# First four levels of a triangular inverse: 128x128 products against stacked 32x32 blocks

## The reference

```python
lower = jnp.where(strict, jnp.einsum('bhncd,bhnmd->bhncm', k_beta, k) * decay, 0.0)
a_mat = lower + jnp.eye(C, dtype=jnp.float32)
rhs = jnp.concatenate([v_beta, k_beta * jnp.exp(g)[..., None]], axis=-1)
sol = lax.linalg.triangular_solve(a_mat, rhs, left_side=True, lower=True, unit_diagonal=True)
```

## Time and profile before

| | |
|---|---|
| median of 3 runs | 1993.72 us (1990.28 to 1998.13) |
| the profiled execution | 1995.55 us |
| its span | 1993.7 us |
| PE busy | 1885.1 us, 95% |
| DVE busy | 1487.0 us, 75% |
| ACT busy | 1073.9 us, 54% |
| POOL busy | 223.7 us, 11% |
| instructions | 30396 |

### The profile page before, as it was taken

How to read it: one execution, slowest core, us unless ns; L and a number is a source line. 1 busy time by engine, 2 the same in 40 slices (tenths; PEclk the granted TensorE clock), 3 DMA queues, 4 the chain that set the end, 5 groups by cost and what they waited for, 6 DMA issues and landing times.

```text
span 1993.7 us, 30396 instructions
## 1 busy us (share of the span) xinstructions
PE 1885.1 (95%) x12080; PEld 1666.1 (84%) x12080; DVE 1487.0 (75%) x2335; ACT 1073.9 (54%) x1753; POOL 223.7 (11%) x182
## 2 busy tenths in 40 slices
PE   6899999988999998999799989998999999989998
PEld 5899788788978887888699978887888789988887
DVE  4655699866567997888777777998787777776565
ACT  5534645564365456555644556445656654456554
POOL 0210111112001111111000001111111100001111
PEclk9999999989999999999899999999999999999999
DMA  5222689522339973555443348894445433344552
GB/s 222 97 107 106 254 342 356 187 104 88 106 110 357 355 277 138 232 211 211 190 149 110 147 169 315 344 362 182 175 174 190 169 127 128 119 178 148 190 186 89
DMA packets 53277, 383.80 MB, mean 193 GB/s; under 512 B 5904, under 2 KB 6032, under 8 KB 6928
## 3 DMA queue, kind: packets, MB, share of 16 engines
q1 hardware_dynamic: 53136, 381.86, 50.9%
HBM read 380.79 MB, written 1.05 MB: 192 GB/s over the span
## 4 chain that ended last, share of the span: by engine, by line
PE 76%; DVE 12%; ACT 6%; issue 4%; DMA 2%; POOL 0%; SPq 0%; DVEq 0%; ACTq 0%
PE quad L492 19%; PE quad L493 10%; PE quad L482 6%; PE quad L483 6%; PE quad L484 6%; PE works L504 4%; PE works L506 4%; PE works L505 4%; ACT w_hi L958 2%; DVE w_lo L1272 2%; DVE mx L1391 2%; DMA raw<-w 2%; DVE mx L1432 1%; PE works L663 1%; PE works L876 1%
## 5 line engine op out<-in xcount | busy, mean ns | idle before, releaser
L1272 DVE TENSOR_TENSOR w_lo<-raw,w_hi 128x1024 fp32r<-128x1024 f32 x572 | 700.5, 1233 | 239.0 <-ACT w_hi L958 237.7
L492 PE MATMUL quad<-h_two,w_hi 128*128 128x512 f32 x2112 | 750.8, 399 | 15.6 <-DVE h_two L1280 9.7
L958 ACT ACTIVATE w_hi<-raw 128x1024 fp32r<-128x1024 f32 x572 | 596.1, 1054 | 206.3 <-PE quad L493 89.9
L493 PE MATMUL quad<-h_two,w_lo 128*128 128x256 f32 x2112 | 594.0, 281 | 0.0
L492 PEld LDWEIGHTS quad<-h_two,w_hi 128*128 128x128 f32 x2112 | 398.1, 189 | 116.9 <-issue 19.7
L493 PEld LDWEIGHTS quad<-h_two,w_lo 128*128 128x128 f32 x2112 | 400.4, 190 | 1.9
L1773 POOL TENSOR_TENSOR g_lo<-hid,g_hi 128x256 fp32r<-128x256 f32 x140 | 177.6, 1270 | 1550.9 <-ACT g_hi L988 1550.9
L482 PE MATMUL quad<-h_two,w_hi 128*128 128x256 f32 x960 | 279.0, 291 | 6.1 <-DVE w_lo L1272 6.1
L483 PE MATMUL quad<-h_two,w_hi 128*128 128x256 f32 x960 | 273.3, 285 | 0.0
L484 PE MATMUL quad<-h_two,w_lo 128*128 128x256 f32 x960 | 273.2, 285 | 0.0
L482 PEld LDWEIGHTS quad<-h_two,w_hi 128*128 128x128 f32 x960 | 185.8, 194 | 9.5 <-issue 8.2
(11 more groups left out here) (404 smaller groups left out, 2355.6 us busy)
## 6 DMA issues: line engine op xcount, KB each, us to landing
raw<-w SPq DMA_DIRECT2D x294, 1024.0 KB, 4.9
mx<-w SPq DMA_DIRECT2D x64, 1024.0 KB, 7.0
par<-p_in SPq DMA_DIRECT2D x2, 1110.0 KB, 7.0
x<-x_in SPq DMA_DIRECT2D x1, 1024.0 KB, 6.6
mx<-bt_in SPq DMA_DIRECT2D x2, 512.0 KB, 5.7
out<-x SPq DMA_DIRECT2D x4, 256.0 KB, 2.5
con<-const_in SPq DMA_DIRECT2D x1, 780.0 KB, 4.6
par<-p_in SPq DMA_DIRECT2D x1, 225.0 KB, 6.8
```

Of the source, the lines that this page charges most:

```text
L492: mm(o, hi, h_two[:, kt, :, :], start=kt == 0, stop=False, skip_group_check=True)
L493: return mm(o[:, 0:T], lo, h_hi[:, kt, :], start=False, stop=kt == DT - 1, skip_group_check=True)
L958: f(w_hi[:, v % SLOTS, :], raw[:, chunk_of_unit[v] % RAWS, (v % 2) * UNIT:(v % 2 + 1) * UNIT], ACT.Copy).then_inc(s_hi_ready, 1)
L1272: v.tensor_tensor(w_lo[:, q % SLOTS, :], raw[:, chunk_of_unit[q] % RAWS, (q % 2) * UNIT:(q % 2 + 1) * UNIT], w_hi[:, q % SLOTS, :].bitcast ...
```

## The change

The first four levels never leave the 32x32 blocks on the diagonal. The new code stacks these: `lt_c`, `xi_c`, `xt_c`, `tt_c` are 128 x 8 x 32, with the diagonal block of quarter q of each matrix on the partitions of that quarter.

- `kk`: DVE copies the four quarters of `lt` into `lt_c`, masks, forms I - mask on 128x256, and makes `xt_c` by a block transpose. Step `level` is gone on PE and ACT. POOL makes all four masked copies at once (128x256 each), and then sets `xt` and half of `x` to zero.
- `lvt`, levels 1 to 4: 32 products of 32x32 into one bank, the quarter as the inner loop; one ACT copy of 128x256.
- `lvx`, levels 1 to 4: 32 products 32x32 with 16 columns, for `xt` alone; DVE subtracts on 128x128 and gets `xi_c` by a block transpose.
- The wait for `s_qk_done` moves from lvt 1 to lvt 5.
- Level 5 reads the stacked blocks. Meanwhile POOL copies the blocks (six copies 32x256, each behind the one before) to their places in `xt` and in `xi64`; lvt 6 waits for four of them and the scan for all.
- `con` has five 32-column masks and a 32-column identity in place of seven 128-column masks.

```diff
-                elif kind == "level":
-                    for c in range(TT):
-                        pe.wait_ge(s_x0_done, 2 * L + c + 1)
-                        pe.wait_ge(s_lt_done, 2 * L + c + 1)
-                        for h, r, cols in heads(c):
-                            last = tr(work[c][:, cols], xi[:, r, :], ident)
-                        last.then_inc(s_pe_x0, 1)
                 elif kind == "lvt" and i < 5:
...
+                    pe.wait_ge(s_pool_lts, 4 * L + i)
+                    if i == 1:
+                        pe.wait_ge(s_x0_done, L + 1)
+                    else:
+                        pe.wait_ge(s_x_upd, 8 * L + i - 1)
+                    for r in range(8):
+                        for q in quarter:
+                            last = mm(work[0][q, 32 * r:32 * r + 32], lts_c[i - 1][q, r, :], xt_c[q, r, :],
+                                      start=True, stop=True)
+                    last.then_inc(s_pe_t, 1)
                 elif kind == "lvx" and i < 5:
...
+                    pe.wait_ge(s_t_sb, 8 * L + i)
+                    if i > 1:
+                        pe.wait_ge(s_xi_ready, 4 * L + i - 1)
+                    o = work[1][:, 0:P].rearrange("p (r g b) -> p r g b", r=8, b=1 << i)
+                    for r in range(8):
+                        for q in quarter:
+                            odd = tt_c[q, r, :].rearrange("p (g e b) -> p g e b", e=2, b=1 << i)[:, :, 1, :]
+                            last = mm(o[q, r], xi_c[q, r, :], odd, start=True, stop=True)
+                    last.then_inc(s_pe_dx, 1)
...
+                elif kind == "lvt" and i < 5:
+                    act.wait_ge(s_pe_t, 8 * L + i)
+                    f(A["t"][:, 0:T], work[0][:, 0:T], ACT.Copy).then_inc(s_t_sb, 1)
...
+                    dve.wait_ge(s_lt_done, 2 * (L + 1))
+                    for q in quarter:
+                        v.tensor_copy(lt_c[q], lt[q, :, q]).then_inc(s_ltc_done, 1)
+                    dve.wait_ge(s_ltc_done, 4 * (L + 1))
+                    v.tensor_tensor(xi_c, lt_c, c_("m", 0, 32).unsqueeze(1).to_broadcast([P, 8, 32]), ALU.mult)\
+                        .then_inc(s_l0_masked, 1)
+                    dve.wait_ge(s_l0_masked, L + 1)
+                    link(v.scalar_tensor_tensor(xi_c, xi_c, -1.0, c_("idc").unsqueeze(1).to_broadcast([P, 8, 32]),
+                                                ALU.mult, ALU.add))
+                    v.transpose(xt_c, xi_c).then_inc(s_x0_done, 1)
...
+                elif kind == "lvx" and i < 5:
+                    dve.wait_ge(s_pe_dx, 8 * L + i)
+                    dve.wait_ge(s_x0_done, L + 1)
+                    odd = xt_c.rearrange("p r (g e b) -> p r g e b", e=2, b=1 << i)[:, :, :, 1, :]
+                    v.tensor_tensor(odd, odd, work[1][:, 0:P].rearrange("p (r g b) -> p r g b", r=8, b=1 << i),
+                                    ALU.subtract).then_inc(s_x_upd, 1)
+                    dve.wait_ge(s_x_upd, 8 * L + i)
+                    v.transpose(xi_c, xt_c).then_inc(s_xi_ready, 1)
...
+                elif kind == "kk":
+                    pool.wait_ge(s_ltc_done, 4 * (L + 1))
+                    for lev in range(1, 5):
+                        v.tensor_tensor(lts_c[lev - 1], lt_c,
+                                        c_("m", 32 * lev, 32 * lev + 32).unsqueeze(1).to_broadcast([P, 8, 32]), ALU.mult)\
                             .then_inc(s_pool_lts, 1)
+                    v.memset(A["xt"], 0.0).then_inc(s_zeroed, 1)
+                    v.memset(A["x"][:, 0:512], 0.0).then_inc(s_zeroed, 1)
+                elif kind == "lvt" and i == 5:
+                    pool.wait_ge(s_zeroed, 2 * (L + 1))
+                    pool.wait_ge(s_x_upd, 8 * L + 4)
+                    pool.wait_ge(s_xi_ready, 4 * (L + 1))
+                    pool.wait_ge(s_qdec_done, L + 1)
+                    for k, (dst, src) in enumerate([(xt[q, :, q], xt_c[q]) for q in quarter[2:]]
+                                                   + [(xi64[q, :, q], xi_c[q]) for q in quarter[:2]]
+                                                   + [(xt[q, :, q], xt_c[q]) for q in quarter[:2]]):
+                        v.tensor_copy(dst, src).then_inc(s_spread, 1)
+                        pool.wait_ge(s_spread, 6 * L + k + 1)
```

More of the change, by code:

```diff
@@ L70 @@
      ("pair", 3), ("lead", 8), ("silu", 3), ("pair", 8), ("lead", 9), ("nsum", 1), ("pair", 9), ("nroot", 1),
-     ("nrow", 1), ("lead", 4), ("kk", 0), ("nrow", 0), ("pair", 4), ("level", 0), ("kq", 0), ("lead", 5),
+     ("nrow", 1), ("lead", 4), ("kk", 0), ("nrow", 0), ("pair", 4), ("kq", 0), ("lead", 5),
      ("silu", 4), ("lvt", 1), ("tokk", 0), ("pair", 5), ("lvx", 1), ("lead", 10), ("silu", 5), ("lvt", 2),
@@ L202 @@
                   ("d", 4), ("b_re", 4 * P), ("b_im", 4 * P), ("c_re", ST * 32), ("c_im", ST * 32)])
-PC, NC = columns([("ident", P), ("triu", P), ("ones", P), ("m", 7 * P), ("pen", P), ("time", T // 2), ("c", 8),
+PC, NC = columns([("ident", P), ("triu", P), ("ones", P), ("m", 5 * 32), ("idc", 32), ("pen", P), ("time", T // 2), ("c", 8),
                   ("final", 8), ("sel", 8)])
@@ L315, in build @@
         qdec = hf[:, 2:4, :].rearrange("p n t -> p (n t)").rearrange("p (n t) -> p n t", t=P)
+        blocks = lambda a: a.rearrange("p (n t) -> p n t", t=32)
+        xi64 = A["x"][:, 0:512].rearrange("p (n t) -> p n t", t=64)
+        tt6 = A["t"][:, 0:512].rearrange("p (n t) -> p n t", t=64)
+        xi_c, xt_c = blocks(A["x"][:, 512:768]), blocks(A["x"][:, 768:1024])
+        tt_c, lt_c, tt5 = (blocks(A["t"][:, k:k + T]) for k in (0, 256, 512))
+        lts_c = [blocks(A["lts"][:, T * k:T * k + T]) for k in range(4)]
+        quarter = [slice(32 * p, 32 * p + 32) for p in range(4)]
         vn0, s_sb = lts[:, 0:4, :], lts[:, 4:8, :]
@@ L377, in build @@
             conv_done th_done silu_done rt_done rs_done pe_nrow qk_ready pe_kk lt_done
-            pe_kq qk_done l0_masked x0_done pe_tokk pe_tokv kd_done vb_done pool_lts
-            pe_x0 x0_sb pe_t t_sb pe_dx
+            pe_kq qk_done l0_masked x0_done ltc_done xi_ready zeroed spread pe_tokk pe_tokv kd_done vb_done pool_lts
+            pe_t t_sb pe_dx
             x_upd z_th c_done pe_u0 vn0_done pe_s s_done pe_w w_done pe_u1
@@ L772, in _ @@
                         for r in range(8):
-                            last = mm(works[up, 2 * p, 32 * r:32 * r + 32], lt[low, r, up], xt[low, r, low],
+                            last = mm(works[up, 2 * p, 32 * r:32 * r + 32], lt[low, r, up], xt_c[low, r, :],
                                       start=True, stop=True)
@@ L1131, in _ @@
                                 .then_inc(s_kd_done, 1)
[L1132 to L1135, removed]
+                elif kind == "lvt" and i < 5:
+                    act.wait_ge(s_pe_t, 8 * L + i)
+                    f(A["t"][:, 0:T], work[0][:, 0:T], ACT.Copy).then_inc(s_t_sb, 1)
                 elif kind == "lvt":
                     for c in range(TT):
[L1138 to L1142 removed]
+                        act.wait_ge(s_pe_t, 8 * L + 2 * (i - 3) + c + 1)
+                        if i == 5:
+                            dst = tt5[64 * c:64 * c + 32, :, :]
                             src = works[64 * c:64 * c + 32, 2 * c, 0:T].rearrange("p (r b) -> p r b", b=32)
                         else:
[L1145 removed]
+                            dst = tt6[0:64, 4 * c:4 * c + 4, :]
                             src = works[0:64, 2 * c, 0:T].rearrange("p (r b) -> p r b", b=64)
@@ L1879 @@
     same = lambda size: (idx[:, None] // size) == (idx[None, :] // size)
-    masks = [same(2 * z) & ~same(z) & (idx[:, None] > idx[None, :]) for z in (1, 2, 4, 8, 16, 32, 64)]
+    masks = [same(2 * z) & ~same(z) & (idx[:, None] > idx[None, :]) for z in (1, 2, 4, 8, 16)]
     future = np.where(idx[None, :] > idx[:, None], BIG, 0.0)
@@ L1883 @@
         "ident": np.eye(P), "triu": (idx[:, None] <= idx[None, :]), "ones": np.ones((P, P)),
-        "m": np.concatenate(masks, axis=1), "pen": -future,
+        "m": np.concatenate([np.tile(m[:32, :32], (4, 1)) for m in masks], axis=1),
+        "idc": np.tile(np.eye(32), (4, 1)), "pen": -future,
         "time": np.broadcast_to(np.arange(BLK)[None, :], (P, BLK)), "c": tiles(a["c_2"][0]),
```

83 lines of the change are left out of this document (21 added, 62 removed).

## The result

The changed kernel takes 1962.12 us (median of 4 runs, 1959.39 to 1967.12) against 1995.93 (4 runs, 1990.28 to 1999.18) of the kernel before: a ratio of 0.9836, 95% interval 0.9803 to 0.987. The profiled execution took 1960.0 us, 35.55 less than that of before; the sum of the prediction was 35.1. The page of the changed kernel: span, busy times, chain by engine, the load of the constants.

The account below looks back on a forecast made before the run. PE was taken as the bound, with 76% of the chain. Per layer 15.8 + 1.0 + 1.3 - 1.0 = 17.1 us, twice 34.2, plus 0.9 = 35.1, giving 1959 against the median; 8-in-10 range 1950 to 1974.

Parts of the forecast that it names:

- the start: Kernel start: the smaller constants load 352 KB less, so the first weights land 0.9 us earlier, once.
- a step is 0.51 + 0.19 = 0.70 us: PE, lvt or lvx of levels 1 to 4: four tiles at once, 0.51 us of instructions plus 0.19 for change of shape.
- A level: PE, levels 1 to 4: each level gains 3.95 us from its two shorter steps, four levels 15.8 us.
- its lower bound of 0.35 us less: PE, lvx: moving only 16 columns might make that step perhaps 0.35 us shorter than 0.70.
- The front: kk to lvt 1: DVE reaches kq's input 1.0 us sooner (bounds 0 and 1.9); first lvt's dropped wait gives 1.3.
- The collision with POOL: DVE's kk: the new multiply and subtract meet POOL's four new masks; 0.7 us added once.
- The wait for qk_done: First lvt: it no longer waits for qk_done, which moves to level 5; 1.3 us gained per layer.
- The wait that the change adds: PE before lvt 2: waits 0.9 to 1.0 us for DVE's level 1 update, behind six convolution taps.
- Rival 1: PE steps: four tiles don't run at once because they write one PSUM bank; step 2.21 us, total 1982.6; chance 0.12.
- Rival 2: PE steps: only two tiles run at once; step 1.20 us, total 1967.5; chance 0.15.
- Rival 3: Levels 2 to 4: DVE becomes the bound, 1 us more before each lvt, price 6 us, total 1965; chance 0.12.
- Rival 4: PE clock: short steps halve the granted clock from lvt 1 to lvt 5; 28 us slower, up to 2022; chance 0.02.

Follow-up runs that it names:

- e1: The changed kernel run again unchanged, as reference for its series; 1960.15 us, ratio 0.9816.
- e9: The changed kernel run again unchanged in a later series, as reference for e10 and e11; 1961.64 us, ratio 0.9831.
- e5: The changed kernel with the wait for qk_done put back in front of the first lvt; 1964.69 us, one run.
- e8: The changed kernel with step lvx 1 moved ahead of pair 5 on every engine; 1954.54 us, one run.
- e2: The changed kernel with the quarter as the outer loop in lvt and lvx, levels 1 to 4 (16 instructions in a row per tile); 1980.09 us, ratio 0.9921.
- e3: The changed kernel with two tiles at a time: quarters 0 and 1 alternating, then 2 and 3; 1967.79 us, ratio 0.9861.
- e7: The changed kernel with three DVE block transposes behind each update instead of one and twelve POOL spread copies instead of six; 1965.89 us, ratio 0.9855.
- e12: The kernel of e8 (lvx 1 ahead of pair 5) timed in five rounds; 1958.57 us, ratio 0.9809.
- e4: The changed kernel with the products of matrices 4 to 7 left out of lvt and lvx, levels 1 to 4; 1966.37 us, one run.
- e10: The changed kernel with lvx 1 ahead of pair 5, level 5's two halves interleaved, and nrow 0 ahead of kk; 1960.97 us, ratio 0.9832.
- e11: The changed kernel with lvx 1 ahead of pair 5 and level 5's two halves interleaved, nrow 0 not moved; 1964.16 us, one run.

## Why the prediction was right, and where a term was off

**The sum.** The time from kk to lvt 5 of layer 1, start to start in the timelines of PE (before: 89.62, 98.14, 104.20, 116.24 and 149.59 us; after: 87.53, 94.58, 99.43, 108.61 and 131.01):

| piece | before | after | gain | forecast |
|---|---|---|---|---|
| kk to kq | 8.52 | 7.05 | 1.47 | 1.0 |
| kq to lvt 1 | 6.06 | 4.85 | 1.21 | 1.3 |
| lvt 1 to lvt 2 | 12.04 | 9.18 | 2.86 | 2.95 |
| lvt 2 to lvt 5 | 33.35 | 22.40 | 10.95 | 11.85 |
| all | 59.97 | 43.48 | 16.49 | 17.1 |

16.49 against 17.1 per layer, and 16.4 and 16.6 by the remainders. With the 0.5 of the start in this trace the changed places give 33.5 us, where the forecast had 35.1. The profiled executions differ by 35.55. The 2 us between come from stretches that the change doesn't touch: 1.3 us between numbers 3 and 9, 25.36 us in before and 24.01 in after, but 25.28 in e1, the changed kernel again; the rest is a balance of gains and losses up to 2.4 us each, mostly where a half-clock stretch falls in one trace and not in the other (over the span after has 80.8 us of them, before 77.7). The agreement of the total to half a microsecond is thus luck. The median was forecast at 1959 and came out at 1962.12. By the medians the difference is 33.8 in the first series, 36.6 with e1 and 33.7 with e9.

**The term that was mis-sized** is "a step is 0.51 + 0.19 = 0.70 us". It is 0.87. The four tiles do run at once, but the 64 starts take 0.56 us where 0.50 was forecast, since the second round over the tiles comes 52 ns after the first and the second half of the starts at 9.3 ns, where I had 32 and 7.9; and 0.31 us are around them where 0.20 was. I had counted only the change of shape at the exit. At the entry the first instruction of a step starts 0.21 us after the last one of the weights, 0.09 more than the weights' pace of 0.12, and the trace of before had this too: L773 starts at 149.59, the weights' last instruction at 149.38. A level therefore gains 3.6 us and not 3.95. That lvx moves only 16 columns gives 0.02 us (0.66 to 0.68); its lower bound of 0.35 us less was far off.

**What balanced it.** The front gained 0.4 us more, 2.68 for 2.3, against 1.0 less in the levels. From the end of the last L1496 (90.28) to the end of the first block transpose (93.36) DVE needs 3.1 us, not 3.5: four copies 1.23 (1.4), mask 0.43 (0.45), L1504 0.86 (0.45, and 0.7 for POOL), transpose 0.45 (0.42 and entry). The collision with POOL seems to be there, in one instruction and not two: L1504 lies wholly inside POOL's masks at 91.61 to 94.85. So does most of L1501, which takes no longer than the same multiply elsewhere; but it began at 91.57, 0.04 us before POOL's first mask. L1504 takes 0.84 to 0.86 us in all 13 traces of the new code, always beside these masks, and no run has it without them: that POOL is the cause is argued and not shown. The wait for qk_done, alone, is worth 1.5 us (e5) for 1.3. (kq came at 94.58 and not at 96 to 97 us, because kk itself, at 87.53 for 89.62, was already 2.1 us earlier in this trace.)

**The wait that the change adds** came where it was forecast, before lvt 2 only, released by DVE behind the taps, 0.96 us for 0.9 to 1.0. e8 takes it away by moving one entry, for 0.85 us.

**The rivals.** Rival 1, four tiles serial because they share a bank: the starts 7 ns apart refute it, and e2 shows the step it would have had. The Trainium skill, TensorEngine Tiling (Array Packing), section Restrictions and Gotchas, states that different row tiles can't access the same PSUM bank at the same time; in this trace four row tiles do, each on its own partitions and in its own columns of the array, with starts 7 ns apart. The fixed cost of some 60 cycles per matmul that the Trainium skill states on the same page, section Performance Considerations, would have made a step 1.8 us, by an estimate from it; measured are 0.87 us with four tiles, and 1.84/64 = 29 ns per instruction only while one tile is used. Rival 2, two at once, is what e3 makes of it: 1.23 us a step (1.20 forecast), and after is faster than that. Rival 3, DVE as the bound: none of the later steps waits, and with two more transposes per level (e7) the pitch is the same. Rival 4, the clock between the levels: after has no time at half clock from kk to lvt 6 in either layer.

**What stays open.** Why one trace has 74 us at half clock and another 105 wasn't settled. Within one kernel (e12) the time falls and rises with the mean clock over 13 us, so part of it is not the program's doing; e4, e7, e10 and e11 were all in the upper part in their traced runs, which may be their changed rhythm or four draws. Nor is it settled why the starts slow down in the second half of a step.

## What to carry to other kernels

Small products in different tiles of the array are nearly free beside each other when consecutive instructions go to different tiles, and cost their full pace when they don't: the order of two loops decides between 0.87 and 2.03 us for the same 64 instructions. Count the way in as well as the way out of such a block, 0.3 us in all here, and let the block be long. Shorter steps on the main engine use up the slack of its helpers, so look for the update that was just in time before, and put its producer ahead of unrelated work in the queue. Moving work only to remove one wait can cost more at the next: nrow 0 ahead of kk saved 0.7 us at lvt 1 and lost 1.44 at lvx 1. Gains of 2 to 5 us in a 1960 us kernel have to be read in the stretch of the trace where they arise, since stretches at half clock move the total by more than that; and inside the stretch, compare pieces whose clock was the same.

## What the runs showed of the hardware

- Four 32x32 tiles on the diagonal write the same PSUM bank at once: starts 7 ns apart, four per 32 ns in the first half of a step, 9.3 ns each in the second; 0.56 us from first to last start and 0.31 us around them (after, e4).
- A VectorE block transpose of 128x256 float32 takes 0.45 us, where a pass with one input over the same size takes 0.35 (L1458); a 32x256 copy 0.28 to 0.31.
- On GpSimd the same 32x256 copy takes 0.39 us, but the first of the six 1.15, together 3.41 us (1.3 each was allowed); setting 128x1024 float32 to zero takes 0.94 and 128x512 0.52 (after).
- A half-clock stretch of 3.4 us between lvt 6 and lvx 6 makes the same work 5.6 us long instead of 4.1 (after against e10 and e11).
- The granted clock differs between executions of one kernel: 0.973 with 1967.71 us and 0.982 with 1955.58 in e12.
